# Moving a kernel's token operands to other SBUF addresses

## What is computed

```python
gate, up = jnp.split(x @ w_gu, 2, axis=-1)      # w_gu 1024 x 5632, four times
y = (jax.nn.silu(gate) * up) @ w_down           # w_down 2816 x 1024, four times
proj = jnp.einsum('bld,dn->bln', h, w_in)       # the first layer's projection
```

## Time and profile before

| | us |
|---|---|
| median of three runs | 1196.64 (1196.5 to 1197.19) |
| span of the profiled execution, first to last instruction | 1195.0 |
| PE (TensorE matmul) busy | 1187.3 (99%), 7956 instructions |
| PEld (weight load) busy | 1089.4 (91%), 7956 |
| DVE (VectorE) busy | 934.7 (78%) |
| ACT (ScalarE) busy | 730.4 (61%) |
| POOL (GpSimd) busy | 77.9 (7%) |
| bytes moved by DMA | 209.92 MB, mean 176 GB/s |

### The profile page before, as it was taken

How to read it: one execution, slowest core, us unless ns; L and a number is a source line. 1 busy time by engine, 2 the same in 40 slices (tenths; PEclk the granted TensorE clock), 3 DMA queues, 4 the chain that set the end, 5 groups by cost and what they waited for, 6 DMA issues and landing times.

```text
span 1195.0 us, 22393 instructions
## 1 busy us (share of the span) xinstructions
PE 1187.3 (99%) x7956; PEld 1089.4 (91%) x7956; DVE 934.7 (78%) x1617; ACT 730.4 (61%) x1211; POOL 77.9 (7%) x91
## 2 busy tenths in 40 slices
PE   9999999999999999999999999999999999999998
PEld 9899999888888999999888889988888989888887
DVE  7766788988876788688988767888876787888853
ACT  7564746666654588567666645666664567666642
POOL 4460000000000000610000000000000000000000
PEclk9999999999999999999999999999999999999999
DMA  8545655554654445115555743655663423555730
GB/s 329 184 142 187 232 189 177 186 208 176 230 214 154 141 170 188 41 36 177 211 178 204 258 151 123 211 176 194 219 239 135 150 91 125 195 205 178 255 131 36
DMA packets 48143, 209.92 MB, mean 176 GB/s; under 512 B 3486, under 2 KB 4908, under 8 KB 43596
## 3 DMA queue, kind: packets, MB, share of 16 engines
q1 hardware_dynamic: 46720, 204.96, 48.7%
q10 hardware_dynamic: 1356, 4.07, 1.0%
HBM read 207.90 MB, written 1.13 MB: 175 GB/s over the span
## 4 chain that ended last, share of the span: by engine, by line
PE 93%; DVE 4%; ACT 1%; issue 1%; DMA 1%; DVEq 0%; SPq 0%; ACTq 0%
PE main L2165 25%; PE main L2167 13%; PE main L2523 13%; PE main L2138 8%; PE main L2139 8%; PE main L2140 8%; PE main L2525 7%; DVE w_lo L1157 1%; PE side L2303 1%; PE main L2566 1%; PE side L2566 1%; PE side L2277 1%; PE main L2682 1%; PE main L2854 1%; PE main L2858 1%
## 5 line engine op out<-in xcount | busy, mean ns | idle before, releaser
L1157 DVE TENSOR_TENSOR w_lo<-raw,w_hi 128x1024 fp32r<-128x1024 f32 (+3 forms) x365 | 466.8, 1287 | 5.0 <-ACT w_hi L594 3.8
L2165 PE MATMUL main<-xs,w_hi 128*128 128x512 f32 x1328 | 461.3, 390 | 0.2 <-DVE xs L1191 0.2
L594 ACT ACTIVATE w_hi<-raw 128x1024 fp32r<-128x1024 f32 (+2 forms) x363 | 402.5, 1111 | 68.3 <-PE main L2140 53.0
L2167 PE MATMUL main<-xs,w_lo 128*128 128x256 f32 x1328 | 374.5, 282 | 0.0
L2165 PEld LDWEIGHTS main<-xs,w_hi 128*128 128x128 f32 x1328 | 249.2, 188 | 53.2 <-DVE w_lo L1157 0.7
L2167 PEld LDWEIGHTS main<-xs,w_lo 128*128 128x128 f32 x1328 | 251.0, 189 | 0.0
L2523 PE MATMUL main<-h_both,w_hi 128*128 128x512 f32 x682 | 236.6, 390 | 0.0
L2525 PE MATMUL main<-h_both,w_lo 128*128 128x256 f32 x682 | 192.3, 282 | 0.0
L2523 PEld LDWEIGHTS main<-h_both,w_hi 128*128 128x128 f32 x682 | 128.0, 188 | 26.8
L2525 PEld LDWEIGHTS main<-h_both,w_lo 128*128 128x128 f32 x682 | 128.9, 189 | 0.0
L2138 PE MATMUL main<-xs,w_hi 128*128 128x256 f32 x368 | 105.4, 286 | 0.0
(11 more groups left out here) (505 smaller groups left out, 1869.6 us busy)
## 6 DMA issues: line engine op xcount, KB each, us to landing
raw<-in_w_gu_a SPq DMA_DIRECT2D x44, 1024.0 KB, 5.2
raw<-in_w_gu_b SPq DMA_DIRECT2D x44, 1024.0 KB, 5.2
raw<-in_w_down_a SPq DMA_DIRECT2D x16, 1408.0 KB, 6.1
raw<-in_w_down_b SPq DMA_DIRECT2D x16, 1408.0 KB, 6.0
raw<-in_w_in SPq DMA_DIRECT2D x15, 1024.0 KB, 5.4
raw<-in_w_in_a SPq DMA_DIRECT2D x13, 1024.0 KB, 5.2
raw<-in_w_gates SPq DMA_DIRECT2D x4, 1024.0 KB, 5.1
raw<-in_w_up SPq DMA_DIRECT2D x4, 1024.0 KB, 5.2
```

Source lines behind the costliest of these rows:

```text
L594: act.activation(w_hi[:, u % RING, 0:n], raw[:, s % RAW, u % 2, 0:n], ACT.Copy).then_inc(hi_ready, 1)
L1157: return dve.tensor_tensor(dst, src, hi.bitcast(F32), ALU.subtract)
L2165: pe.matmul(bank[:, :], piece(w_hi, u, k), xs[:, k], start=k == 0, stop=k == KC - 1, skip_group_check=True)
L2167: ins = pe.matmul(bank[:, 0:SEQ], piece(w_lo, u, k), xs_hi[:, k], start=False, stop=k == KC - 1, skip_group_check=True)
```

## The change

It alters three numbers in `program`. `xs` starts right behind `x` and no longer 32 bytes further, `xg` starts 64 bytes and no longer 32 below where it would just end at `raw`, and everything behind `free0` starts 32 bytes further.

```diff
         x, at = place("x", (nc.sbuf_base + 31) // 32 * 32, [P, KC, SEQ])
-        xs, _ = place("xs", at + 32, [P, KC, 2, SEQ], F32R)
+        xs, _ = place("xs", at, [P, KC, 2, SEQ], F32R)
         xs_hi, xs_lo = xs[:, :, 0], xs[:, :, 1]
         at_raw = at + 4 * 2 * KC * TOK
-        xg, at = place("xg", at_raw - 32 - 4 * 2 * KC * X_ROW, [P, 2, KC, X_ROW], F32R)
+        xg, at = place("xg", at_raw - 64 - 4 * 2 * KC * X_ROW, [P, 2, KC, X_ROW], F32R)
...
-        free0 = at
+        free0 = at + 32
```

## The result

| | before | after |
|---|---|---|
| median of the runs shown | 1196.59 us (1196.5 to 1197.19, four runs) | 1212.35 us (1211.17 to 1213.56, four runs) |
| ratio | | 1.0131, interval 1.0118 to 1.0143 |
| span of the profiled execution | 1195.0 us | 1209.5 us |
| granted clock | 1.000 | 0.999 |

The change costs 15.8 us, and 14.5 us of it are in the two spans. The forecast had the sign, and it looked in the right quantity, the time from one matmul's start to the next; it had 6.4 us of size and a range that ended at 1211.0, so the result lies outside it.

A forecast was written before the change was run, and what follows sets the result against it. PE's matmul pitches were taken to bound the kernel: 4.8 + 1.8 - 0.2 = 6.4 us for `xs` and `xg`, nothing for the second region, so 1196.64 + 6.4 = 1203.0 us. The range ran from 1188.5 to 1211 us.

The forecast's parts named there:

- What bounds the kernel: Whole kernel: PE busy 99% of the span at full clock, hardly waiting, so time is a sum of matmul pitches.
- I put the excess on the moving one: Full-rate matmuls: the moving operand's start at 0 costs 3.6 ns at 512 columns, 1.0 ns at 256; the stationary place hardly matters.
- the forecast's own test: Value units should stay near 233 ns; a clear fall would mean the stationary start was the cost.
- part 1: `xs` and `xg` at 0: long matmuls 4.8 us, triples 1.8 us, value units 0.2 us less; 6.4 us slower.
- that no row has: Matmuls with both operands at 0: a case the earlier trace lacked, allowing no cost or twice the sum as bounds.
- Part 2 at nothing: Second region, `h_both` included, moved from 32 to 64: 0 us, from half-rate float32 rows taking 0.86 us at both places.
- The bound of 3.4 us: Second region: at full rate 64 may cost what 0 costs, 3.4 us more, or as much less.
- The cover: VectorE and ScalarE accesses to moved tiles: PE hardly ever waits for these engines, so costed at nothing.
- Scatter: Triples at equal addresses modulo 128: 1.2 ns between two stretches, kept as having nothing to do with a tile's place.
- The place makes no difference: Rival for all moved tiles: moving stream and weight load don't meet in SBUF, 1196.6 us; chance 25%.
- Start at 32 costs: Rival for all full-rate token-moving matmuls: multiples of 64 are better, 6.7 us gained at 1 ns each, 1189.9 us; chance 28%.
- Both at 0 collide hard: Upper end for `xs`/`xg` plus the second region's bound: 16.2 us, 1212.8 us; within the slower case's 47%.

The follow-up runs named there:

- e3_all_plus_32: Kernel before with everything, weights and tokens alike, starting 32 bytes further (weights at 32, tokens at 64): 1196.85 us, ratio 0.9999.
- f4_lo_weights_at_32: Changed kernel with `w_lo` moved to 32, tokens left where the change put them: 1199.86 us, ratio to before 1.0026.
- m1_places_alone: Separate small kernel, TensorE alone on zeros, eight places of `w_lo` by eight of the tokens, `w_hi` at 0, two shuffled passes: pairs about 340 to 353 ns.
- g1_tokens_plus_128: Kernel before with tokens 128 bytes from where they were, weights unmoved: 1198.92 us, ratio 1.0018.
- n1_lo_64_tokens_64: Against before: `w_lo`, `xs` and the second region at 64, `w_hi` at 0, `xg` at 32: median 1198.35 us, ratio 1.0002.
- the first four experiments: Against before: `xs`/`xg` at 0 alone, 1204.41 us; second region at 64 alone, 1201.43; everything 32 bytes further, 1196.85; weights 64 with tokens 0, 1209.37.

## Why the prediction was right or wrong

**What bounds the kernel** held. PE's share, its waits and the clock are as before, and the change shows in the pitches alone.

**"I put the excess on the moving one"** is the step that failed. It took from the earlier trace rows that a moving start at 0 costs, whatever the stationary operand does, with a price per matmul. `e3_all_plus_32` moved every moving start and changed nothing; `f4_lo_weights_at_32` moved no token tile and changed 12.5 us. What counts is where the weights and the tokens lie against each other. The value units tell the same, in the forecast's own test: with both operands at 0 they fell from 233.0 to 226 ns. It had said that this would mean that part 1 is wrong. It had also said that the stationary start would then be the cost, and that isn't it either: with `w_lo` alone at 32 (`f4_lo_weights_at_32`) and the tokens still at 0 they take 233 again. The earlier trace rows measured a pair of places (weights 0 moving, tokens 32 standing still), and the prediction read it as one of them.

The earlier trace rows could not carry its part either. Its stationary operand starts at many places, so its 117.9 ns are a mean over many distances; that a mean is ordinary says nothing of any one of them.

**Part 1, the size.** Forecast 6.4 us for `xs` and `xg`; alone it measured 7.6 (with two stretches of `xs` at 353.3), and inside the change 6.4 + 2.8 + 2.0 less 0.7 = 10.5 us (with three). The pairs' 4.8 us became 6.4: 353.3 ns in three of four stretches, where the forecast had 350.3. Its 3.15 us for nine pairs was seen nowhere: it was 3.12 or 3.18. The triples' 1.8 us became 4.8, because both operands at 0 give 120.0 ns a matmul and not 118.3. That case was named as one "that no row has", and only the upper bound had anything for it.

**Part 2 at nothing** was the other failed step: 4.5 us on `h_both`. Its rows, are float32 matmuls at half the rate, and carried nothing for the full-rate pairs; and they compared 64 with 32 without asking where the stationary operand was. The bound of 3.4 us was itself short by 1.1 us. The triples of the second region, some 900 matmuls, did stay near nothing, within 1 us by their pitches.

**The cover.** VectorE's and ScalarE's instructions did not grow, as said: the splits of weights on L1157 have a median of 1219 ns before and 1218 after, and `m1_places_alone` shows the pitches with both engines idle.

**Scatter.** The prediction set the 1.2 ns between the two stretches of the earlier trace rows aside as nothing to do with place. It was half right: equal places can give different pitches. But it was not noise around one value. The same 353.3 and 346.7 return for hundreds of pairs, and a mean of such stretches is what a single window doesn't show.

**The rivals.** *The place makes no difference* is out: place alone moved the time from 1186.4 to 1213.2 us. The Trainium skill, in "SBUF — State Buffer", section "Who interferes with whom", gives TensorE two independent read ports, one for the moving operand and one for the weight load, and the box on cachelines in "Door 1" gives lines of 16 bytes. These runs disagree with the rule that the prediction made of the two, that 0, 32 and 64 are alike: with the weights at 0 they gave 353.3 or 346.7, 346.7, and 353.3 ns a pair. Whether the ports meet is not shown. *Start at 32 costs* is out too: with the weights at 0, none of the eight places tried was better for the pairs than 32. *Both at 0 collide hard* came near the size, 1212.8 us, by luck: its sum doubles part 1 and adds a bound for part 2, and both terms are off (12.8 for 10.5 us, 3.4 for 4.5). The triples with both operands at 0 do cost more than a mixed pair of places did, but `h_both` at 64 lost as much a pair as `xs` at 0.

**What stays open.** That the places of weights and tokens act together is shown. That only their distance counts is shown for the pairs and for two common shifts, 32 and 64 bytes; the 128 bytes of `g1_tokens_plus_128` show that it isn't simply the distance modulo 128 for the triples. How they act on each other, inside the memory or the engine, isn't shown. Nor is the rule by which a distance gives its pitch, or what in a break decides between two pitches: at one and the same break the changed kernel went over to 353.3 in one execution and stayed at 346.7 in the other. It wasn't tried to force one of them, by a wait at a chosen point for instance. And `w_hi` and `w_lo` were never given all 64 combinations.

## What to carry to other kernels

Where TensorE bounds and its matmuls are short, the start addresses of the weights and of the moving tile are a setting to be measured, as a pair: here moves of 16 to 80 bytes took a pair of matmuls from 340 to 360 ns, and the kernel over 2%. A small kernel with TensorE alone that runs every combination in two shuffled orders finds the candidates in one run. A place whose two passes disagree is a poor one to try; one whose passes agree still has to be confirmed in the whole kernel, since of the two fastest such here one held (48 with 112) and one held only in part (64 with 64). Before reading the cost of an operand off a row, ask what the other operand of that row was doing.

## What the runs showed of the hardware that was not expected

- The steady mean pitches of a pair in the whole kernels are few: 340.0, 346.7, 350.0, 353.3 and 360.0 ns. At 2.4 GHz (the granted clock was 0.999 to 1.000) these are 816, 832, 840, 848 and 864 clocks, all multiples of 8, with 768 columns to stream. The one exception is `h_both` in `f4_lo_weights_at_32`, 348.9 ns or 837 clocks; the small kernel has places between, such as 348.9 and 348.5 for `w_lo` at 64 with tokens at 32.
- One and the same place can run at two pitches for hundreds of pairs: 353.3 and 346.7 (tokens at 0), 360.0 and 346.7 (tokens at 16), 340.0 and 350.0 (`w_lo` and tokens at 64). Where it changed, it did so only where the row of pairs was broken. Runs of such a kernel stand apart by one stretch, 2.2 us or more (1211.2 and 1213.5 for after; 1192.4 to 1198.7 for `n1_lo_64_tokens_64`), while before, with its one pitch, stayed between 1196.6 and 1198.1 in the 14 runs beside the first four experiments.
- Moving the tokens by a whole 128 bytes left the pairs at 346.7 ns and lengthened the triples by 2.8 to 5.1 ns.
- In the value units, with the weights moving and tokens standing still, both at 0 is the best case seen (226 ns, against 233 with only `w_lo` off it, at 32), and for the triples with the tokens moving it is as slow as any case seen (120.0 ns).
